# A two-role decoder layer on eight cores: the recurrent branch's convolution and gates of two equal tiles in one operation each

## The chip, the cores and the metric

The kernel runs on all eight cores of one Trainium2 chip. The cores do not talk to each other: each pair of cores serves one of the four sequences of the batch. The metric is the device time of the slowest core, in microseconds, and the number given for a kernel is the median of several executions.

## The reference

One decoder layer, x of shape (4, 4096, 1024) in float32:

```
h      = RMSNorm(x)
[u_pool | u_rnn | u_gate | g_pool | g_rnn] = h @ W_in
y_pool = PoolMixer(u_pool) @ W_pool_out
v      = conv4(u_rnn)                         # causal, depthwise, 4 taps
r, i   = sigmoid(v @ w_a + b_a), sigmoid(v @ w_x + b_x)     # 8 heads of 128x128
a      = exp(-8 r softplus(-lam));  h_t = a_t h_(t-1) + sqrt(1 - a_t^2) i_t v_t
y_rnn  = (h * gelu(u_gate)) @ W_rnn_out
x      = x + (sigmoid(g_pool) y_pool + sigmoid(g_rnn) y_rnn) @ W_o
x      = x + SwiGLU(RMSNorm(x));   out = RMSNorm(x)
```

## The kernel before

**Two roles.** Channels lie on the partitions, tokens on the free axis. An even core has role a: it computes the first 2240 tokens of its sequence. An odd core has role b: it computes the last 1856 tokens, but because the recurrence runs over the whole sequence it also runs norm, projection, convolution, gates and scan of the recurrent branch (and only these) over the 2240 tokens before its own. This part is called the prefix. Role a cuts its tokens in two chunks of three tiles each (256, 412, 396 and 344, 500, 332). Role b cuts the prefix in tiles of 256, 496, 496, 496, 496, taken in groups of 2, 2 and 1 tiles, and its own tokens in chunks of 508, 508 and 460, 380.

**The recurrent branch** is `rnn_group`, called for each of the eight heads (j = 0 to 7) and each group or chunk. For each tile of the group: eight matmuls of w + 4 columns into one PSUM bank (`proj`, L705); ScalarE evicts the bank with the fourth tap and the bias into `v` (L745); VectorE adds the other three taps, one operation each, reading the bank (L757); GpSimd, or ScalarE for some heads, casts `v` to bf16 (L765, L763); two matmuls with the head's gate weights (L770), and one tanh each on ScalarE into `th` and `wi` (L780). After the tiles of the group, one operation over all its columns for each of: exp (L788), square (L792 or L795), square root (L798), the product with v (L815), the product with the root (L822), and the scan (L828). Exp and tanh share one activation table, the square root needs another, so ACT_TABLE_LOADs stand between them.

**The rest of a chunk** is projections for the gelu (L993), pool and merge gates (L1012, L1027), the output projections, and the channel mixer, all matmuls through `mm_group` (L705) with one eviction or two each.

**Who sets the order.** Nothing is ordered by hand. Every operation gets a key, `base + step * block + toff * tile + off[block]`, from the tables in `ROLES`; a planner (`Planner.run`) walks a modelled time, lets each engine take the ready operation of lowest key, gives it SBUF and one of eight PSUM banks, and so fixes each engine's order, which the engines then follow strictly with semaphore waits. All numbers of `ROLES` come from a search over that model.

**The head.** Both roles begin with the same operations: the load of the first tile `xt` (SP queue), its norm, and on the GpSimd queue the loads of the projection weights of head 0, of all gate weights, and of heads 1 to 3:

```
            if j == 0:
                head.append(self.load("pool", rg, lambda: rg.tensor[:], dr["rg"], 128 * 2048 * 4, K, "rg"))
```

Weights are read as float32 and written as bf16 (a 512 KB `keep_rg` is 1 MB of reads). After the head each engine reads the role and branches into the stream of its role.

## Time and profile before

| | |
|---|---|
| median of 3 runs | 1024.84 us (1024.12 to 1025.46) |
| the profiled execution | 1024.35 us |
| its span on the slowest core, core 3 (role b) | 1022.8 us |
| PE, DVE, ACT, POOL busy on core 3 | 924.4, 591.4, 556.7, 336.8 us |
| mean granted TensorE clock, role a / role b | 0.985 / 0.951 to 0.954 |

The span runs from the first to the last instruction of a core; 1.55 us of the profiled execution lie outside the slowest span. PE is busy 90% of core 3's span, but the share is uneven: the first third has idle stretches and a clock below full, the last two thirds none. VectorE and ScalarE are the other way round.

### The profile page before, as it was taken

The page shows a single profiled execution, that of the slowest core. Times are in us where ns is not written, and L with a number is a line of the kernel's source. Part 1 is how long each engine was busy: PE and PEld are TensorE (multiplying, and loading weights), DVE is VectorE, ACT ScalarE, POOL GpSimd, SP SyncE. Part 2 cuts the span into 40 slices and gives each one's busy share as a digit, 9 for nine tenths or more (in the row PEclk, how much of TensorE's full clock was granted, in tenths as well). Part 3 has the DMA queues.
Part 4 walks back from the last instruction along what each step waited for, and adds up shares of the span by engine and source line. Part 5 has one row for each costly group of instructions (what it writes and reads, how often), then busy time and mean ns, then how long its engine had stood idle before and what let it go on. Part 6 is the DMA issues. An engine that isn't in the chain of part 4 may idle for free.

```text
span 1022.8 us, 13708 instructions; the slowest of 8 cores (1016.8 to 1022.8 us)
## 1 busy us (share of the span) xinstructions
PE 924.4 (90%) x4484; PEld 446.6 (44%) x4484; DVE 591.4 (58%) x798; ACT 556.7 (54%) x804; POOL 336.8 (33%) x347
## 2 busy tenths in 40 slices
PE   2378688698978999999999999999999999999995
PEld 1134233233433444444444444444555555555553
DVE  2179998999999867844253544533644452222235
ACT  2579997989889942548264938611722351111112
POOL 2438593778655641151001122112251211000000
PEclk8579789899989999999999999999999999999998
DMA  8921452003644276768403257255939175910003
GB/s 176 242 69 33 160 93 42 12 1 55 116 82 87 38 192 118 160 98 150 82 8 56 39 80 141 44 101 123 253 69 212 30 129 108 211 41 2 1 1 135
DMA packets 42765, 96.88 MB, mean 95 GB/s; under 512 B 3776, under 2 KB 19264, under 8 KB 42560
## 3 DMA queue, kind: packets, MB, share of 16 engines
q0 software_dynamic: 23904, 63.45, 36.1%
q1 hardware_dynamic: 18784, 32.48, 10.6%
q8 instruction: 40, 0.66, 0.2%
q14 instruction: 37, 0.30, 0.1%
HBM read 151.75 MB, written 7.60 MB: 156 GB/s over the span
## 4 chain that ended last, share of the span: by engine, by line
PE 78%; ACT 9%; issue 5%; POOL 3%; DVE 2%; DMA 2%; ACTq 0%; DVEq 0%; SPq 0%; POOLq 0%
PE bank L705 74%; PE bank L770 2%; PE bank L667 2%; DMA wu<-w_in 2%; ACT th L780 1%; DVE v L757 1%; ACT q L798 1%; POOL sq L638 1%; ACT th L788 1%; ACT v L745 1%; ACT L798 1%; ACT L780 1%; DMA xt<-xT 1%; POOL vb L765 1%; ACT wi L780 0%
## 5 line engine op out<-in xcount | busy, mean ns | idle before, releaser
L705 PE MATMUL bank<-h,wf 128*128 128x508 bf16 (+2 forms) x1408 | 280.7, 358 | 0.0
L705 PEld LDWEIGHTS bank<-h,wf 128*128 128x128 bf16 x1408 | 136.5, 97 | 139.9 <-issue 0.8
L757 DVE SCALAR_TENSOR_TENSOR v<-bank,keep_cst,v 128x496 f32<-128x496 f32 (+3 forms) x200 | 128.8, 683 | 32.4 <-POOL v L754 13.4
L705 PE MATMUL bank<-h,wu 128*128 128x500 bf16 (+4 forms) x576 | 130.1, 381 | 16.3 <-DMA wu<-w_in 11.0
L1084 DVE TENSOR_TENSOR ff<-tf,bank 128x508 bf16<-128x508 f32 (+2 forms) x88 | 55.7, 634 | 147.9 <-PE bank L705 123.5
L705 PE MATMUL bank<-ff,wz 128*128 128x508 bf16 (+2 forms) x704 | 139.5, 359 | 0.0
L1079 ACT ACTIVATE tf<-bank 128x508 f32<-128x508 f32 (+2 forms) x88 | 48.8, 557 | 137.8 <-PE bank L705 134.4
L652 ACT ACTIVATE sq<-x 128x508 f32<-128x508 f32 (+2 forms) x56 | 32.9, 590 | 125.3 <-DVE x L1096 97.4
L705 PEld LDWEIGHTS bank<-ff,wz 128*128 128x128 bf16 x704 | 68.9, 98 | 68.6 <-issue 0.5
L705 PEld LDWEIGHTS bank<-h,wu 128*128 128x128 bf16 x576 | 58.7, 103 | 83.9 <-issue 32.9
L765 POOL CAST vb<-v 128x496 bf16<-128x496 f32 (+3 forms) x68 | 61.1, 905 | 61.4 <-DVE v L757 53.3
L770 PE MATMUL bank<-vb,keep_rg 128*128 128x496 bf16 (+4 forms) x144 | 43.2, 381 | 33.4 <-ACT th L780 10.1
L515 POOL DMA_DIRECT2D wf<-wfi x44 | 23.8, 549 | 147.1 <-PE bank L705 106.0
L795 POOL TENSOR_TENSOR q<-th 128x752 f32<-128x752 f32 (+3 forms) x31 | 56.9, 1843 | 37.8 <-ACT th L788 18.9
L682 DVE SCALAR_TENSOR_TENSOR h<-xt,keep_cst,bank 128x500 bf16<-128x500 f32 (+4 forms) x72 | 45.8, 686 | 30.8 <-ACT bank L674 29.7
L745 ACT ACTIVATE v<-bank,keep_cst 128x496 f32<-128x496 f32 (+3 forms) x72 | 51.7, 732 | 19.1 <-PE bank L705 18.0
L705 PE MATMUL bank<-h,wa 128*128 128x508 bf16 (+2 forms) x256 | 56.6, 367 | 3.0 <-ACT th L780 1.7
L1096 DVE TENSOR_TENSOR x<-bank,x 128x508 f32<-128x508 f32 (+2 forms) x32 | 20.4, 639 | 64.9 <-PE bank L705 64.6
L705 PE MATMUL bank<-h,wg 128*128 128x508 bf16 (+2 forms) x256 | 55.2, 367 | 2.8 <-ACT th L780 1.9
L780 ACT ACTIVATE th<-bank,keep_hb 128x496 f32<-128x496 f32 (+3 forms) x72 | 44.8, 639 | 22.1 <-PE bank L770 21.8
L638 POOL TENSOR_TENSOR sq<-sq,sq 128x1000 f32<-128x1000 f32 (+2 forms) x18 | 41.9, 2330 | 36.9 <-ACT sq L623 30.3
L705 PE MATMUL bank<-h,wb 128*128 128x508 bf16 (+2 forms) x256 | 53.9, 363 | 0.0
(103 smaller groups left out, 1311.7 us busy)
## 6 DMA issues: line engine op xcount, KB each, us to landing
wf<-wfi POOLq DMA_DIRECT2D x44, 512.0 KB, 9.5
wz<-wfo POOLq DMA_DIRECT2D x16, 704.0 KB, 10.1
xt<-xT SPq DMA_DIRECT2D x16, 500.0 KB, 8.6
wu<-w_in POOLq DMA_DIRECT2D x16, 256.0 KB, 13.7
xt<-xT SPq DMA_DIRECT2D x8, 512.0 KB, 21.1
wa<-w_in POOLq DMA_DIRECT2D x16, 256.0 KB, 5.9
wg<-w_in POOLq DMA_DIRECT2D x16, 256.0 KB, 5.4
wb<-w_in POOLq DMA_DIRECT2D x16, 256.0 KB, 5.5
```

What stands on the lines that cost most here:

```text
L638: self.ew(adds, 2 * w, key, lambda e, t=t: e.tensor_tensor(out=sq.tensor[:], in0=sq.tensor[:], in1=t.tensor[:], op=ALU.add), [sq, t], [sq] ...
L652: g.op("act", c_act(w), key, lambda e: e.activation(out=s.tensor[:], in_=x2[cc // 2].tensor[:, cc % 2, :], func=AF.Square), rd=[(x2[cc // ...
L682: g.op("dve", c_dve(w) + 0.04, key + 0.1 * kc, lambda e, kc=kc, b=b, o=o, h=h: e.scalar_tensor_tensor(out=o.tensor[:, h, :], in0=b.tensor[ ...
L705: last = e.matmul(p.tensor[:, 0:n], lhsT=wap(kc), rhs=rhs(kc), start=(kc == 0), stop=(kc == K - 1))
L745: g.op("act", c_act(w, 2), k, lambda e, p=p, o=o, w=w: e.activation(out=v.tensor[:, o:o + w], in_=p.tensor[:, HALO:HALO + w], func=AF.Iden ...
L757: g.op("dve", c_dve(w), k, lambda e, p=p, o=o, w=w, s=s: e.scalar_tensor_tensor(out=v.tensor[:, o:o + w], in0=p.tensor[:, HALO - s:HALO - ...
L765: cast = lambda e, vb=vb, o=o, w=w: e.tensor_copy(out=vb.tensor[:], in_=v.tensor[:, o:o + w])
L770: g.op("pe", c_mm(w) + 0.05, k + 1 + 0.3 * q, lambda e, pg=pg, q=q, vb=vb, w=w: e.matmul(pg.tensor[:, 0:w], lhsT=self.rg.tensor[:, q, j, : ...
L780: g.op("act", c_act(w, 1), k + 1 + 0.3 * q, lambda e, pg=pg, out=out, hcol=hcol, w=w: e.activation(out=out(), in_=pg.tensor[:, 0:w], func= ...
L795: g.op("pool", 0.09 + 0.0018 * W, k, lambda e: e.tensor_tensor(out=q2.tensor[:], in0=th.tensor[:], in1=th.tensor[:], op=ALU.mult), rd=allp ...
L1079: g.op("act", c_act(w), kf, lambda e, pg=pg, th=th, w=w: e.activation(out=th.tensor[:], in_=pg.tensor[:, 0:w], func=AF.Silu), rd=[pg], wr= ...
L1084: g.op("dve", c_dve(w), kf, lambda e, pu=pu, th=th, fb=fb, w=w: e.tensor_tensor(out=fb.tensor[:], in0=th.tensor[:], in1=pu.tensor[:, 0:w], ...
```

## The change

It does four things.

1. Where a group has exactly two tiles of the same width, and neither the PSUM variant (`ps`), nor the ScalarE tap (`tap`), nor the PE convolution (`pec`) is in use for the head, a new function `rnn_pair` takes the place of the per-tile loop. Both tiles' projections go to the two halves of a pair of neighbouring PSUM banks, and the first eviction, each of the three taps, the cast and each tanh become one operation over both tiles. The matmuls stay as they are.
2. The planner can give out an even-numbered pair of neighbouring banks (`ps2`). Single banks are taken by preference from pairs whose other bank is in use.
3. The gate weights are stored by head, and loaded in four pieces of two heads. Only the first piece is in the head; the other three are loads of their own with keys.
4. Every number of `ROLES` is searched anew. Role b's prefix groups become 1, 2, 2 tiles (256; 496, 496; 496, 496), and its own second chunk 420, 420; the last chunk's `ps` goes from 1 to 0, and its `tap` from 8 heads to 2. The tile widths of role a stay (256, 412, 396 and 344, 500, 332), and so does the split at token 2240.

```
+    def find_bank(self, b, t):
+        free = [self.bank_live[i] is None and self.banks[i][0] <= t for i in range(8)]
+        if b.space == "ps2":
+            c = [(max(self.banks[i][0], self.banks[i + 1][0]), i) for i in range(0, 8, 2) if free[i] and free[i + 1]]
+        else:
+            c = [(self.bank_live[i ^ 1] is None, self.banks[i][0], i) for i in range(8) if free[i]]
+        return min(c)[-1] if c else None
...
-        self.rg = rg = self.buf("keep_rg", [2, 8, 128], BF16)
+        self.rg = [self.buf("keep_rg", [2, 2, 128], BF16) for _ in range(4)]
...
             if j == 0:
-                head.append(self.load("pool", rg, lambda: rg.tensor[:], dr["rg"], 128 * 2048 * 4, K, "rg"))
+                head.append(self.load_rg(0, K))
...
+    def load_rg(self, i, key):
+        b = self.rg[i]
+        return self.load("pool", b, lambda: b.tensor[:], self.dr["rg"][:, 2 * i:2 * i + 2], 128 * 512 * 4, key, "rg")
...
-        for i, (h, w, part) in enumerate(tiles):
+        both = len(tiles) == 2 and tiles[0][1] == tiles[1][1] and not (ps or on[2] or on[5])
+        if both:
+            self.rnn_pair(j, tiles, wu, key, toff, v, th, wi, kk_vb)
+        for i, (h, w, part) in enumerate([] if both else tiles):
...
+    def rnn_pair(self, j, tiles, wu, key, toff, v, th, wi, cast):
+        g, cst = self.g, self.cst
+        w = tiles[0][1]
+        two = lambda b: b.tensor[:].rearrange("p (t w) -> p t w", t=2)
+        p = self.banks("ps_u")
+        for i, (h, _, part) in enumerate(tiles):
+            self.mm_group(p, w + HALO, wu, lambda kc, h=h: h[kc // 2].tensor[:, kc % 2, 0:w + HALO],
+                          [(h[kc // 2], kc % 2) for kc in range(8)], key + toff * i, "u", wap=lambda kc: wu.tensor[:, kc, :], half=i)
+        k = key + toff
+        pk, vk = [(p, 0), (p, 1)], [(v, 0), (v, 1)]
+        g.op("act", c_act(2 * w, 2), k, lambda e: e.activation(
+            out=two(v), in_=p.tensor[:, :, HALO:HALO + w], func=AF.Identity,
+            scale=cst.tensor[:, C_CW + 24 + j:C_CW + 25 + j], bias=cst.tensor[:, C_CB + j:C_CB + j + 1]),
+            rd=pk + [cst], wr=vk, tag="v0")
+        for s in (1, 2, 3):
+            g.op("dve", c_dve(2 * w), k, lambda e, s=s: e.scalar_tensor_tensor(
+                out=two(v), in0=p.tensor[:, :, HALO - s:HALO - s + w],
+                scalar=cst.tensor[:, C_CW + 8 * (3 - s) + j:C_CW + 8 * (3 - s) + j + 1], in1=two(v),
+                op0=ALU.mult, op1=ALU.add), rd=pk + [cst] + vk, wr=vk, tag="cv")
+        vb = self.buf("vb", [2 * w], BF16)
...
+        for q, hcol, dst in ((0, 0, th), (1, 8, wi)):
+            pg = self.banks("ps_g")
+            for i in range(2):
+                g.op("pe", c_mm(w) + 0.05, k + 1 + 0.3 * q, lambda e, pg=pg, q=q, i=i: e.matmul(
+                    pg.tensor[:, i, 0:w], lhsT=self.rg[j // 2].tensor[:, j % 2, q, :], rhs=vb.tensor[:, i * w:i * w + w], start=True, stop=True),
+                    rd=[vb, self.rg[j // 2]], wr=[(pg, i)], tag="gt")
+            g.op("act", c_act(2 * w, 1), k + 1 + 0.3 * q, lambda e, pg=pg, dst=dst, hcol=hcol: e.activation(
+                out=two(dst), in_=pg.tensor[:, :, 0:w], func=AF.Tanh, scale=0.5,
+                bias=self.hb.tensor[:, hcol + j:hcol + j + 1]), rd=[(pg, 0), (pg, 1), self.hb], wr=[(dst, 0), (dst, 1)], table=TANH, tag="th")
...
+        base, step = (P["rnn"][0] if P else prm["keys"][0]["rnn"])[:2]
+        for i in range(1, 4):
+            self.load_rg(i, base + step * 2 * i - prm["lead"])
...
-        prefix=[256, 496, 496, 496, 496], groups=[2, 2, 1], own=[[508, 508], [460, 380]], wp=261.84, window2=107.54,
+        prefix=[256, 496, 496, 496, 496], groups=[1, 2, 2], own=[[508, 508], [420, 420]], wp=322.07, window2=277.53,
```

## Rows read from the trace of the kernel before

**Rows 1.** Spans and granted clock by core: even cores role a, odd role b

```profile
core 0: 1017.9 us, clock 0.985
...
core 3: 1022.8 us, clock 0.951
...
core 6: 1021.7 us, clock 0.985
```

**Rows 2.** Busy time by stretch, core 3 (role b): stretch, length, engines, PEclk, DMA

```profile
20.00:60.00 40.00, 13.61 (x44) 6.23 (x42) 11.38 (x22) 20.69 (x30) 20.47 (x17) 0.50 0.91 227
60.00:342.00 282.00, 235.96 (x988) 99.77 (x987) 264.53 (x297) 249.60 (x349) 187.65 (x149) 0.91 0.31 62
342.00:1000.00 658.00, 656.67 (x3366) 329.10 (x3366) 298.23 (x442) 278.58 (x413) 125.69 (x173) 1.00 0.51 97
```

**Rows 3.** Who PE waited for, core 3, 60 to 342 us: total, times, longest

```profile
PE bank L770 <- ACT th L780: 10.1, 6, 3.7
PE bank L770 <- DVE v L757: 8.5, 5, 4.2
```

**Rows 4.** Groups of VectorE instructions by form, core 3: busy us, mean ns

```profile
L757 DVE SCALAR_TENSOR_TENSOR v<-bank,keep_cst,v 128x496 f32<-128x496 f32 x96 | 65.2, 720 | 3.8 <-ACT v L745 3.7
...
L828 DVE TENSOR_TENSOR_SCAN wi<-th,q 128x752 f32<-128x752 f32 x8 | 16.6, 2073 | 0.5 <-POOL q L822 0.5
...
L757 DVE SCALAR_TENSOR_TENSOR v<-bank,keep_cst,v 128x256 f32<-128x256 f32 x24 | 11.1, 475 | 12.7 <-ACT v L745 6.3 <-ACT ab L582 5.6
...
L828 DVE TENSOR_TENSOR_SCAN wi<-th,wi,q 128x496 f32<-128x496 f32 x8 | 11.0, 1372 | 0.0
```

**Rows 5.** VectorE in order of time, core 3: start, us

```profile
211.76 2.00 DVE L757 SCALAR_TENSOR_TENSOR v<-bank,keep_cst,v 128x496 f32<-128x496 f32 x3
```

**Rows 6.** Groups of ScalarE instructions by form, core 3

```profile
L745 ACT ACTIVATE v<-bank,keep_cst 128x496 f32<-128x496 f32 x32 | 24.0, 763 | 4.8 <-PE bank L705 4.6 <-POOL acc L640 0.2
L780 ACT ACTIVATE th<-bank,keep_hb 128x496 f32<-128x496 f32 x32 | 21.4, 673 | 6.7 <-PE bank L770 6.6
...
L780 ACT ACTIVATE th<-bank,keep_hb 128x256 f32<-128x256 f32 x8 | 3.8, 473 | 1.8 <-PE bank L770 1.6
```

**Rows 7.** ScalarE in order of time, core 3

```profile
203.16 0.68 ACT L780 ACTIVATE wi<-bank,keep_hb 128x496 f32<-128x496 f32 x1
203.72 0.77 ACT L745 ACTIVATE v<-bank,keep_cst 128x496 f32<-128x496 f32 x1
204.36 0.61 ACT L1012 ACTIVATE tp<-bank 128x508 f32<-128x508 f32 x1
```

**Rows 8.** Busy time by stretch, core 6 (role a)

```profile
20.00:60.00 40.00, 25.18 (x99) 13.57 (x97) 12.30 (x23) 17.39 (x28) 12.90 (x26) 0.77 1.08 193
60.00:115.00 55.00, 52.85 (x351) 33.76 (x350) 51.68 (x70) 46.59 (x87) 20.19 (x23) 1.00 0.21 41
115.00:1000.00 885.00, 885.00 (x5515) 539.63 (x5514) 451.18 (x687) 373.65 (x622) 178.38 (x223) 1.00 0.44 88
```

**Rows 9.** Start of core 6 in order of time, POOL and PE

```profile
8.90 0.53 POOL L515 DMA_DIRECT2D keep_rg<-rg  x1
...
18.80 1.89 PE L705 MATMUL bank<-h,wu 128*128 128x260 bf16 x8 [5.81 <-DMA wu<-w_in]
...
21.36 0.53 POOL L515 DMA_DIRECT2D wq<-w_in  x1 [10.35 <-issue]
...
25.05 1.89 PE L705 MATMUL bank<-h,wu 128*128 128x260 bf16 x8 [4.37 <-DMA wu<-w_in]
...
30.19 0.56 POOL L765 CAST vb<-v 128x256 bf16<-128x256 f32 x1
...
38.68 3.11 PE L667 MATMUL bank<-sq,keep_ones 128*128 128x416 f32 x4 [1.76 <-ACT sq L623]
```

**Rows 10.** Start of core 0 (role a) in order of time, POOL and PE

```profile
14.47 0.53 POOL L515 DMA_DIRECT2D wq<-w_in  x1 [3.28 <-issue]
...
24.11 1.89 PE L705 MATMUL bank<-h,wu 128*128 128x260 bf16 x8 [4.26 <-DMA wu<-w_in]
...
34.01 3.11 PE L667 MATMUL bank<-sq,keep_ones 128*128 128x416 f32 x4 [1.65 <-ACT sq L623]
```

More of the change, by code:

```diff
@@ L164, in can_alloc @@
                 continue
-            if b.space == "ps":
-                if not any(self.bank_live[i] is None and self.banks[i][0] <= t for i in range(8)):
+            if b.space != "sb":
+                if self.find_bank(b, t) is None:
                     return False
@@ L169, in can_alloc @@
                 n += b.nbytes
-        if room and any(b.space == "ps" and b.left is not None for b in o.bufs):
+        if room and any(b.space != "sb" and b.left is not None for b in o.bufs):
             room = 0
@@ L179, in do_alloc @@
             b.left = b.uses
-            if b.space == "ps":
-                c = [(self.banks[i][0], i) for i in range(8) if self.bank_live[i] is None and self.banks[i][0] <= t]
-                _, i = min(c)
-                self.bank_live[i] = b
-                b.off = i
-                extra += self.banks[i][1]
+            if b.space != "sb":
+                i = b.off = self.find_bank(b, t)
+                for x in range(i, i + (2 if b.space == "ps2" else 1)):
+                    self.bank_live[x] = b
+                    extra += self.banks[x][1]
             else:
@@ L198, in finish_refs @@
                 b.dead = max(u.end for u in b.users)
[L199 to L200 removed]
+                if b.space != "sb":
                     us = {}
@@ L203, in finish_refs @@
                         us[u.eng] = u
-                    self.banks[b.off] = (b.dead + self.prm["bank_lag"], list(us.values()))
+                    for x in range(b.off, b.off + (2 if b.space == "ps2" else 1)):
+                        self.bank_live[x] = None
+                        self.banks[x] = (b.dead + self.prm["bank_lag"], list(us.values()))
                 elif b.name.startswith("keep"):
```

91 lines of the change are left out of this document (48 added, 43 removed).

## The prediction

> **What bounds the kernel now.** I read the spans of all cores first, because the metric is the slowest core and the two roles run different programs. Role b ends at 1022.8 us; of role a, core 0 ends at 1017.9, and core 6 at 1021.7 [rows 1]. So role b sets the time, but only 1.1 us ahead of the slowest core of role a. Whatever the change takes off role b beyond 1.1 us counts only if role a comes down too. This is the main fact of the case.
>
> Next, busy time by stretch. In role b PE is full from 342 to 1000 us (656.7 of 658); before that it is not: from 60 to 342 us it is busy 236 of 282 us at a clock of 0.91, while VectorE is busy 264.5 and ScalarE 249.6 [rows 2]. That stretch is bound by VectorE, with ScalarE close behind: the prefix and the first chunk's convolution, gates and scans. What PE waits for in it is work of these two: the gate matmuls wait for a tanh to free a bank (10.1 us) and for the taps (8.5 us) [rows 3]. From 20 to 60 us role b has the opposite picture: VectorE is busy 11.4 of 40 us and the DMA engines 91% [rows 2]. Before 342 us a microsecond less of VectorE work is a microsecond less of PE loss; behind it nothing is to be had.
>
> In role a PE is full from 115 to 1000 us (885 of 885 us). Its loss lies at the start: 14.8 us idle and a clock of 0.77 from 20 to 60 us, and 2.1 us idle from 60 to 115 [rows 8].
>
> **The merged operations (role b only).** Role a always has three tiles in a group, so nothing merges there. In role b two prefix groups, the first own chunk and six heads of the second chunk merge: 8 + 8 + 8 + 6 = 30 pairs. The last six lie where PE is full, and are worth nothing on the path. The other 24 each save 3 tap operations on VectorE and 1 eviction and 2 tanh on ScalarE. The columns stay, so only the fixed part of an operation is saved. VectorE: 496 columns take 720 ns, 256 take 475, so a column costs (720 - 475) / 240 = 1.02 ns and the fixed part of a duration is 720 - 506 = 0.21 us [rows 4]. But neighbours overlap: three taps in a row take 2.00 us, which is 0.64 us from start to start, of which 0.51 is columns and 0.13 fixed [rows 5]. Bounds: 72 x 0.13 = 9.4 us and 72 x 0.21 = 15.1 us. I take 9.4, since the engine is full and works at the spacing. ScalarE: a column of the tanh costs (673 - 473) / 240 = 0.83 ns [rows 6], 0.41 us for 496; the spacing is 0.56 us for a tanh and 0.64 for the eviction [rows 7], so fixed parts of 0.15 and 0.23 us: 48 x 0.15 + 24 x 0.23 = 12.7 us. Both engines of that stretch are relieved by about the same, so neither takes the other's place. I expect the saving to come through: -9.4 us.
>
> What does a merge cost? The first tap waits for the second tile's projection, and the banks are held longer. A pair of u banks is held for 8 matmuls, one eviction of about 1.2 us and three taps of about 1.2 us: some 7 us, while VectorE has 282 us for 24 pairs, or 11.8 us for each. One pair of u banks, at most two, and two pairs for the gates fit into eight banks. No row shows such an operation across two banks; below, the nearest is that it runs at the same 1.02 ns a column (what I take); above, that it splits at the bank border and costs its fixed part twice, and then the saving is nothing. The trace also speaks for a loss here, in that PE's longest wait is for a tanh to free a bank (3.7 us) [rows 3]. By the Trainium skill ("Perfetto Trace Analysis", Optimizing Tensor Performance) independent matmul groups should rotate through different banks, so that one's evacuation overlaps the next group's matmuls; a pair halves the number of places to rotate through. That speaks against this change, and if each of the 24 pairs cost one such wait, the sum would be a loss. Rows 3 put all waits for a tanh of the gate matmuls at 10.1 us in 282, so I give it a small chance.
>
> **The groups 1, 2, 2.** The first group is now the 256-column tile alone, so its exp, root and scan can run while the DMA engines still bring the next tiles, between 20 and 60 us, where VectorE is idle 28.6 us [rows 2]. The scan alone of these columns costs (2073 - 1372) ns x 8 heads = 5.6 us of VectorE [rows 4], now in the full stretch. Between 0 and 5.6 us; GpSimd's squares for the second tile stand in the same queue, so I take half, -2.8 us. Role b comes to 1022.8 - 9.4 - 2.8 = 1010.6 us.
>
> **The gate weights in four.** 384 of the 512 KB leave the head. On core 6 the weights of head 0 are used at 18.80 us and those of head 1, which wait for their DMA, at 25.05 [rows 9]: 6.25 us for 512 + 256 KB. Half of that is gone: -3.1 us for the second projection, and with it for what follows. The pieces come back as three loads of 128 KB each; the fixed issue is 0.53 us each on the GpSimd queue [rows 9], in front of casts, 1.6 us together at most. Is the gain passed on? On core 6 the first cast waits until 30.19 us behind weight issues that begin at 21.36, because GpSimd stood still for 10.35 us after the head; on core 0 it stood 3.28 us [rows 9, 10]. Core 6 is late by 4.7 us at the second tile's statistics (38.68 against 34.01), and still by 3.8 at the end [rows 1, 9, 10]. So a microsecond at role a's start is about a microsecond at its end, and the spread of its four cores is made in the head. If the stall lasts as long as the head's loads are under way, fewer bytes shorten it; if not, the gain stays 0 for that core. I take 3.1 us for all of role a: core 0 at 1014.8, core 6 at 1018.6.
>
> **The order searched anew, role a.** No row prices it. Its room is what PE loses between 20 and 115 us: 14.8 + 2.1 us idle, and 0.23 x 25.2 = 5.8 us of slow clock, together 23 us, of which the load above takes 3. Below: nothing is regained, and a new order can lose as much as the 3.8 us by which one core of the same order now trails. Above: half of the remaining 20. I take -3, because at 24 us PE still waits for a DMA while the second tile's statistics, which need no weights, stand behind it in the order [rows 9]. Role a's slowest core: 1015.6 us.
>
> **Sum.** Slowest core max(1010.6, 1015.6) = 1015.6, and the 1.5 us outside the span: 1017.1, so 1017. The profiled execution took 1024.35 us with a span of 1022.8, 0.5 below the median of the runs; the sum is made against it. The time is then role a's, and 5 us of role b's gain are hidden.
>
> **Rivals.**
> - *Role b keeps the end.* A merge returns little: operations that cross a bank border pay twice, or PE waits for two free neighbours. With 0 to 3 us of saving role b ends at 1019.8 to 1022.8, the time 1021.3 to 1024.3. For it: no such operation in the trace. Against: VectorE is busy 94% there, so removed instructions must show. Taken at 1022.
> - *Role a does not move.* The stall after the head is not made by the loads, and the weights are only read in another order: core 6 stays at 1021.7, the time 1023.2, within 0.2%. For it: two cores with the same head stand 3.3 and 10.4 us. Against: the wait for the second weights is a DMA wait on both.
> - *Both gain more.* The new order fills role a's start (half of 20 us): role a 1008.6, role b 1010.6 or lower, the time 1008 to 1012.
> - *Slower: neighbouring banks.* PE, with operations of both tiles in one bank pair, waits at the gates of each pair. The margin is 12.2 us of saving and 2.05 us more up to 0.2% over the median: at 14.3 / 24 = 0.6 us a pair it is slower. At the 1.7 us that a wait for a tanh lasts today (10.1 / 6) [rows 3] it would be +40.8 - 12.2 = +28.6 if all pairs met it, and with half of them +8, a time of 1033. This is what the rule of the Trainium skill on rotating through banks (named above) would come to here.
>
> **How the numbers follow.** Role a sets it near 1017: 0.50 (1012 to 1021). Role b keeps the end: 0.15. Role a does not move: 0.12. Both gain more: 0.13. Slower by the banks, or by an order of role a that loses over 3 us: 0.10. About 0.2% (2.05 us) is what a measurement can tell from no change, so below 1022.8 is faster: 0.50 + 0.13 + two thirds of 0.15 + a small part of 0.12 = 0.75; within 0.2%: 0.14; slower 0.11. The range takes in most of "both gain more" and ends where slower begins to be likely: 1007 to 1024.
>
> **What would show it.** Right: on odd cores, half as many operations at the taps, of 992 columns, at 1.2 to 1.25 us each, and PE full from about 330 us instead of 342; the odd cores' spans below the even ones'; on even cores the second projection at about 21 to 22 us. Wrong: taps of 992 columns at 1.4 us, which is twice 720 ns; long waits of L705 or L770 for a tap or tanh; PE idle behind 342 us in role b; even cores at 1017 and more.

## The result and the profile after

The change makes the kernel slower: 1041.65 us, the median of 6 executions (1040.20 to 1042.72), beside 1024.91 us before. The ratio is 1.0160, with a 95% interval of 1.0147 to 1.0173. The forecast was 1017 us (1007 to 1024). Where "role a" or "role b" is given a time below, it is the mean span of the four even or the four odd cores over the executions of that kernel; such a mean repeats within some 1.5 us (one and the same program of role a gave 1014.1 and 1012.6 in z1 and z3 below), single terms of that size are at its edge, and the kernel before itself stood 2 to 3 us higher beside z4 and z5 than elsewhere. Executions in which the cores of one die ran slower are left out everywhere. By these means role a goes from 1018.6 to 1020.7, and role b from 1021.3 to 1037.2 us.

The spans of the profiled execution after (1041.87 us), by core:

```profile
core 0: 1027.1 us, clock 0.982
...
core 3: 1040.3 us, clock 0.949
...
core 6: 1022.7 us, clock 0.986
```

All of the loss is role b's: core 3 ends 17.5 us later than in [rows 1]. Role a has not come down on core 6 (1021.7 before) and core 0 is 9 us later in this execution, though role a's mean is only 2.1 us up. The stall of GpSimd behind the head, which stood on core 6 before [rows 9], stands on core 0 this time (3.28 us there before [rows 10]):

```profile
21.64 0.53 POOL L527 DMA_DIRECT2D wu<-w_in  x1 [10.34 <-issue]
```

The same three stretches of core 3 as in [rows 2]:

```profile
20.00:60.00 40.00, 10.56 (x50) 6.50 (x50) 12.78 (x25) 22.41 (x33) 24.12 (x25) 0.63 0.82 173
60.00:342.00 282.00, 236.26 (x975) 98.75 (x976) 251.81 (x218) 229.49 (x272) 153.81 (x123) 0.90 0.34 72
342.00:1000.00 658.00, 647.45 (x3290) 320.63 (x3288) 305.84 (x408) 276.38 (x381) 122.23 (x157) 0.99 0.48 95
```

VectorE is busy 12.7 us less in the second stretch and ScalarE 20.1 us less, as a merge should make it; but PE is busy no more than before (236.3 against 236.0). The engines were relieved and the stretch was not shortened. Behind 342 us, PE is now idle 10.5 of 658 us, where it was idle 1.3. The merged operations themselves, core 3, 60 to 342 us, VectorE by form:

```profile
L876 DVE SCALAR_TENSOR_TENSOR v<-bank,keep_cst,v 128x992 f32<-128x992 f32 x48 | 58.2, 1240 | 2.2 <-ACT v L871 1.3
L847 DVE TENSOR_TENSOR_SCAN wi<-th,wi,q 128x992 f32<-128x992 f32 x16 | 44.0, 2754 | 8.6 <-POOL q L841 8.5
...
L834 DVE SCALAR_TENSOR_TENSOR wi<-wi,v 128x992 f32<-128x992 f32 x16 | 23.4, 1459 | 1.3 <-ACT wi L892 1.3
```

A tap of 992 columns across two banks takes 1240 ns, in the window that the prediction gave (1.2 to 1.25 us): no operation pays twice at a bank border. What stands below it is new: the scan of 992 columns takes 2754 ns, and the 16 scans together are kept 8.5 us by GpSimd's product L841. The same two operations before, same view and stretch (these rows stand in none of the groups above):

```profile
L828 DVE TENSOR_TENSOR_SCAN wi<-th,wi,q 128x992 f32<-128x992 f32 x8 | 19.1, 2400 | 0.0
...
L815 DVE SCALAR_TENSOR_TENSOR wi<-wi,v 128x992 f32<-128x992 f32 x8 | 10.1, 1277 | 0.0
```

**Where role b's time went.** The last product `gl` (L838 before, L857 after) of role b's first own chunk is the point behind which VectorE no longer holds PE. Before it starts at 364.5 us. After, the timeline of core 3, VectorE and then PE, shows it at 375.3:

```profile
372.85 2.33 DVE L847 TENSOR_TENSOR_SCAN wi<-th,keep_hst,q 128x1016 f32<-128x1016 f32 x1
375.29 1.22 DVE L857 TENSOR_TENSOR gl<-wi,gl 128x1016 bf16<-128x1016 f32 x1
...
369.75 1.66 PE L721 MATMUL bank<-h,wb 128*128 128x508 bf16 x7
376.76 5.48 PE L721 MATMUL bank<-gl,wr 128*128 128x508 bf16 x15 [5.34 <-DVE gl L857]
```

PE has nothing left to do in its order that does not need `gl`, and stands 5.34 us: the chain runs through VectorE up to here. The windows from 20 us to this point, and from it to 1000 us, before and then after:

```profile
20.00:364.50 344.50, 272.07 (x1136) 116.27 (x1134) 291.44 (x330) 291.42 (x409) 218.87 (x175) 0.87 0.39 83
364.50:1000.00 635.50, 634.17 (x3261) 318.82 (x3260) 282.70 (x431) 257.45 (x382) 114.94 (x163) 1.00 0.51 97
```

```profile
20.00:375.30 355.30, 275.23 (x1152) 117.64 (x1152) 290.51 (x259) 279.38 (x341) 191.46 (x156) 0.87 0.39 80
375.30:1000.00 624.70, 619.04 (x3161) 308.24 (x3162) 279.93 (x391) 248.89 (x345) 108.71 (x147) 1.00 0.50 98
```

The span after is 17.5 us longer: 10.8 us up to this point and 6.7 us behind it. Up to it VectorE is busy 291.4 us before and 290.5 after: the saving on the taps (9.7 us, 108.7 against 87.8 + 11.2) was given back inside other operations. And it is idle 53.1 us before, 64.8 after. What lies behind the point is settled further down, by z1. Who VectorE waited for up to it, after:

```profile
DVE h L698 <- ACT bank L690: 13.2, 2, 12.6
DVE wi L847 <- POOL q L841: 11.3, 3, 5.0
DVE v L776 <- ACT ab L598: 10.9, 1, 10.9
DVE v L776 <- ACT v L764: 8.5, 3, 6.3
DVE wi L834 <- ACT wi L892: 5.8, 4, 2.9
```

And three of the same waits before, 20 to 364.5 us:

```profile
DVE h L682 <- ACT bank L674: 24.0, 4, 17.4
DVE v L757 <- ACT ab L582: 5.6, 1, 5.6
DVE wi L828 <- POOL q L822: 2.8, 3, 2.3
```

Of the 11.7 us more of idle time, 8.5 are the scans' wait for a GpSimd product (2.8 to 11.3). The waits for ScalarE are 4.3 us more in all (46.2 to 50.5): the first tap waits longer (5.6 to 10.9), the norm of the later tiles less (24.0 to 13.2). The experiments ask what of all this is the merge, the pieces, the order, and the rule for single banks, which the prediction did not cost.

### The profile page after: what moved, and what is told of

Same layout as the page of the kernel before. It is cut to its first block, busy times and chain, and to the rows that moved or that the text cites. A ratio compares the mean times of both kernels' runs of the same rounds, so it can differ in the third digit from the quotient of the medians.

```text
span 1040.3 us, 13139 instructions; the slowest of 8 cores (1021.5 to 1040.3 us)
## 1 busy us (share of the span) xinstructions
PE 929.2 (89%) x4484; PEld 445.8 (43%) x4484; DVE 592.5 (57%) x694; ACT 540.7 (52%) x705; POOL 303.2 (29%) x312
## 3 DMA queue, kind: packets, MB, share of 16 engines
q1 hardware_dynamic: 18784, 32.48, 10.4%
## 4 chain that ended last, share of the span: by engine, by line
PE 78%; ACT 7%; DVE 6%; issue 5%; POOL 2%; DMA 2%; DVEq 0%; ACTq 0%; SPq 0%; POOLq 0%
PE bank L721 75%; DMA wu<-w_in 1%; DVE wi L847 1%; DVE h L698 1%; PE bank L889 1%; PE bank L683 1%; POOL sq L654 1%; ACT q L817 1%; ACT wi L892 1%; ACT th L892 1%; DVE v L876 1%; ACT th L807 1%; DMA xt<-xT 1%; DVE q L841 0%; ACT L817 0%
## 5 line engine op out<-in xcount | busy, mean ns | idle before, releaser
L721 PE MATMUL bank<-h,wf 128*128 128x508 bf16 (+1 forms) x1408 | 280.8, 358 | 2.9 <-DVE h L698 1.9
L1142 DVE TENSOR_TENSOR ff<-tf,bank 128x508 bf16<-128x508 f32 (+1 forms) x88 | 55.8, 637 | 175.9 <-PE bank L721 140.2
L721 PE MATMUL bank<-h,wu 128*128 128x500 bf16 (+3 forms) x576 | 131.2, 385 | 23.7 <-DMA wu<-w_in 11.4
L721 PE MATMUL bank<-ff,wz 128*128 128x508 bf16 (+1 forms) x704 | 139.5, 359 | 0.4 <-issue 0.2
L876 DVE SCALAR_TENSOR_TENSOR v<-bank,keep_cst,v 128x992 f32<-128x992 f32 (+2 forms) x90 | 107.4, 1216 | 13.5 <-ACT v L871 11.1
L814 POOL TENSOR_TENSOR q<-th 128x992 f32<-128x992 f32 (+2 forms) x31 | 52.7, 1701 | 59.8 <-ACT th L807 46.5
L841 POOL TENSOR_TENSOR q<-q,wi 128x992 f32<-128x992 f32 (+3 forms) x24 | 50.0, 2091 | 47.0 <-ACT q L817 35.4
L721 PE MATMUL bank<-h,wb 128*128 128x508 bf16 (+1 forms) x256 | 55.7, 370 | 8.1 <-ACT th L892 6.6
L834 DVE SCALAR_TENSOR_TENSOR wi<-wi,v 128x992 f32<-128x992 f32 (+3 forms) x40 | 48.7, 1223 | 18.4 <-ACT wi L892 12.6
L721 PE MATMUL bank<-gl,wr 128*128 128x508 bf16 (+1 forms) x256 | 53.7, 369 | 5.7 <-DVE gl L857 5.3
L721 PE MATMUL bank<-h,wg 128*128 128x508 bf16 (+1 forms) x256 | 56.0, 374 | 1.6 <-ACT wi L892 1.0
L721 PE MATMUL bank<-h,wa 128*128 128x508 bf16 (+1 forms) x256 | 54.5, 359 | 0.1
## 6 DMA issues: line engine op xcount, KB each, us to landing
wz<-wfo POOLq DMA_DIRECT2D x16, 704.0 KB, 10.9
```

Source lines behind the costliest of these rows:

```text
L721: last = e.matmul(p.tensor[:, 0:n] if half is None else p.tensor[:, half, 0:n], lhsT=wap(kc), rhs=rhs(kc), start=(kc == 0), stop=(kc == K ...
L814: g.op("pool", 0.09 + 0.0018 * W, k, lambda e: e.tensor_tensor(out=q2.tensor[:], in0=th.tensor[:], in1=th.tensor[:], op=ALU.mult), rd=allp ...
L834: g.op("dve", c_dve(w), k, lambda e, o=o, w=w, x=x: e.scalar_tensor_tensor(out=x(), in0=x(), scalar=1.0, in1=v.tensor[:, o:o + w], op0=ALU ...
L841: self.ew(on[1], W, k + 2, lambda e: e.tensor_tensor(out=q2.tensor[:], in0=q2.tensor[:], in1=wi.tensor[:], op=ALU.mult), [q2] + xk, [q2], "b")
L876: g.op("dve", c_dve(2 * w), k, lambda e, s=s: e.scalar_tensor_tensor(out=two(v), in0=p.tensor[:, :, HALO - s:HALO - s + w], scalar=cst.ten ...
L1142: g.op("dve", c_dve(w), kf, lambda e, pu=pu, th=th, fb=fb, w=w: e.tensor_tensor(out=fb.tensor[:], in0=th.tensor[:], in1=pu.tensor[:, 0:w], ...
```

## The experiments

### The merge and the pieces, each by itself

*x1* keeps the order of after and issues each merged operation per tile, back to back. *x5* does the same with finer waits: each tile's operation waits only for its own tile. *x3* exchanges the first two weight loads in the GpSimd queue. *y2* puts the pieces alone into the kernel before, the three late ones right behind the head.

```
# x1 (the eviction, the cast and the tanh alike)
-            g.op("dve", c_dve(2 * w), k, lambda e, s=s: e.scalar_tensor_tensor(
-                out=two(v), in0=p.tensor[:, :, HALO - s:HALO - s + w],
...
+            g.op("dve", c_dve(2 * w), k, lambda e, s=s: [e.scalar_tensor_tensor(
+                out=two(v)[:, i, :], in0=p.tensor[:, i, HALO - s:HALO - s + w],
...
# x5
+        o = first[m.idx] = Op(m.eng, m.dur / 2, m.key, lambda e, f=f: f(e, 0))
+        m.fn = lambda e, f=f: f(e, 1)
# x3
+    pl.order["pool"][pos[0]], pl.order["pool"][pos[1]] = b, a
# y2
-                head.append(self.load("pool", rg, lambda: rg.tensor[:], dr["rg"], 128 * 2048 * 4, K, "rg"))
+                head.append(self.load("pool", rg, lambda: rg.tensor[:, 0:2], dr["rg"][:, 0:2], 128 * 2048 * 4, K, "rg"))
...
+        pl.order["pool"].insert(at + i - 1, o)
```

> The order of the kernel after, with every merged operation (eviction, taps, cast, two tanh) issued as one for each tile, back to back, in the same place; the matmuls, banks, loads and all else stay. Theory 1, the merge gains on VectorE as forecast and something else loses: the spans of role b (odd cores, 1039.5 to 1040.3 in the kernel after) grow by about 24 heads x 3 taps x 0.13 to 0.20 us = 9 to 14 us on VectorE, less what still waits for other things: 1046 to 1055. Theory 2, the merge itself is what costs (a tile waits for its neighbour): the same places and waits are kept here, so the span stays within 3 us of 1040 or falls.

> The kernel after with each merged operation issued as one for each tile in the same place, as in x1_undone_in_place (role b 1048.7 in the mean), but now each tile's operation waits only for its own tile: the eviction of the first tile for its own projection, its taps for its own eviction, its gate matmuls for its own cast, its tanhs for its own gate matmuls. Theory 1, what a pair costs is its number of operations and columns, not that a tile waits for its neighbour: role b is within 2 us of x1. Theory 2, the waiting for the neighbour is what the order lost by: role b is 5 us or more below x1, which is then a cost of the merge that x1 does not show.

> The kernel after with the first two weight loads exchanged: the weights of head 1, which role b projects first, are issued ahead of head 0's. All orders on the engines stay. In the kernel after they land at 25.01 us and the first eviction of role b starts at 28.52. Theory 1, the late start is carried to the end: the first eviction starts 5 us earlier and role b ends at 1034 to 1036. Theory 2, the slack of the later stages takes it up: the first eviction starts earlier and the spans of role b stay at 1038 to 1041. Role a, which projects head 0 first, may lose 2 to 3 us and stays below role b.

> The kernel before with only the gate weights loaded in four pieces: the first where the whole load stood, the other three right behind the four weight loads of the start; every order on the engines, and all else, stays. Theory 1, the prediction's: head 1's weights land 3 us earlier and role a ends up to 3 us earlier (1015 to 1017 where the kernel before has 1017.5 to 1021), role b 1 us or less. Theory 2, the pieces only trade places with what is loaded beside them: the second projection starts 1 to 2 us earlier, the pieces for the later heads or the weights behind them land later, and the spans of both roles stay within 1 us.

| kernel | ratio to before (95%) | role a | role b |
|---|---|---|---|
| x1, per tile, waits of the pair | 1.0248 (1.0224 to 1.0272) | 1020.3 | 1048.7 |
| x5, per tile, waits of the tile | 1.0206 (1.0188 to 1.0224) | 1019.9 | 1041.0 |
| x3, head 1's weights first | 1.0141 (1.0119 to 1.0162) | 1022.4 | 1035.1 |
| y2, pieces in the kernel before | 0.9995 (0.9985 to 1.0005) | 1018.7 | 1019.9 |

Beside after's 1037.2 for role b, fewer operations are worth 11.5 us (x1), which is between the two bounds for VectorE (9.4 and 15.1); x1 also undoes the merges on ScalarE and GpSimd. But 7.7 us of that is paid back because a pair waits for both tiles (x1 to x5), so the merge's net worth in this order is 3.8 us. (With each kernel against the runs of before made beside it, the three numbers are 10.9, 6.8 and 4.1.) The order was searched with the pairs in it, and x1 and x5 keep it and the pairs of banks: in an order searched without them the merge may be worth something else. The taps of x1, same view as above:

```profile
L876 DVE SCALAR_TENSOR_TENSOR v<-bank,keep_cst,v 128x496 f32<-128x496 f32 x96 | 64.2, 722 | 3.1 <-ACT v L871 2.2
```

*x3*: the new order asks first for the weights that land second. The first projection of core 3, after and then x3:

```profile
25.25 4.87 PE L721 MATMUL bank<-h,wu 128*128 128x260 bf16 x24 [11.43 <-DMA wu<-w_in]
```

```profile
18.79 1.89 PE L721 MATMUL bank<-h,wu 128*128 128x260 bf16 x8 [5.24 <-DMA wu<-w_in]
24.45 1.89 PE L721 MATMUL bank<-h,wu 128*128 128x260 bf16 x8 [3.77 <-DMA wu<-w_in]
```

6.5 us earlier at the start is 2.1 us at the end. (1035.1 lies within the first theory's 1034 to 1036, but that was reckoned from the profiled execution of after, 1039.5 to 1040.3; from the mean it is less than half of the 5 us.) *y2*: the pieces alone are worth nothing measurable for the kernel; role b gains 1.4 us, which is at the edge of what can be told, and role a nothing (+0.4). In the profiled executions the second projection of the four even cores starts at 24.8 us in the mean before and at 22.5 in y2, but the second tile's statistics (L667 before) start at 35.7 before and 35.6 in y2. Core 0 and core 6 of y2, GpSimd and span:

```profile
20.01 1.59 POOL L1167 DMA_DIRECT2D keep_rg<-rg  x3 [8.68 <-issue]
15.14 1.59 POOL L1167 DMA_DIRECT2D keep_rg<-rg  x3 [3.88 <-issue]
core 0: 1023.3 us, clock 0.983
core 6: 1018.1 us, clock 0.985
```

The two cores have changed places: with a stall of 8.7 us in place of 3.3 core 0 ends 5.4 us later than before, with 3.9 in place of 10.4 core 6 ends 3.6 us earlier. In these traces the stall falls on another core in another execution, the end of a core of role a follows it, and the smaller load does not take it away.

### GpSimd and VectorE

*c1* (from after) and *c2* (from before) take from GpSimd the reading of its operands: squares and casts become memsets, products and sums have 8 columns. Values are therefore wrong in both, and GpSimd is also busy for less time (60 to 342 us: 79.4 us in place of 153.8 in c1, 84.1 in place of 187.7 in c2). *c3* shortens only the two products that stand beside the longest scan.

```
# c1, c2
-            g.op("pool", 0.09 + 0.0018 * W, k, lambda e: e.tensor_tensor(out=q2.tensor[:], in0=th.tensor[:], in1=th.tensor[:], op=ALU.mult),
+            g.op("pool", 0.09 + 0.0018 * W, k, lambda e: e.memset(q2.tensor[:], 0.01),
...
# c3
+        if o.idx in (713, 755):
...
+            o.fn = lambda e, q=q, x=x: e.tensor_tensor(out=q.tensor[:, 0:8], in0=q.tensor[:, 0:8], in1=x.tensor[:, 0:8], op=ALU.mult)
```

> The kernel after with GpSimd's reading left out: its squares and casts are memsets of the same size, its products and sums have 8 columns (so the values are not those of the reference); every order and wait stays. Theory 1, the operations of VectorE that only touch SBUF are stretched by GpSimd's and this eats the merge's gain: the scans of 992 columns fall from 2.75 us to about 2.3, VectorE's busy time in 60 to 342 us by 10 us or more, and role b ends below 1032, a fall at least 5 us larger than that of the same cut in the kernel before. Theory 2, the stretch is no matter: the fall is at most 3 us larger than in the kernel before.

> The same cut in the kernel before. Theory 1 (the stretch is a matter of the kernel after): the scans, 2.40 us for 992 columns, fall to about 2.3, and role b (1022.8) ends at 1018 to 1022. Theory 2: it falls by as much as the kernel after with the cut.

> The kernel after with only two of GpSimd's products (the two beside one scan of 992 columns in role b, at 309.5 and 314.0 us of core 3, 2.3 us each) cut to 8 columns; nothing else changes (so two heads' values are wrong). In the kernel after that scan takes 6.54 us where another of its size beside no work of GpSimd takes 2.27. Theory 1, VectorE and GpSimd take turns at SBUF and VectorE's operation waits inside its own time: the scan falls to 2.3 us and role b ends 3 to 4.5 us earlier (1035 to 1037 where the kernel after has 1039.5 to 1040.3). Theory 2, the scan is slow for another reason or the delay is taken up later: it stays long, or it falls and role b ends within 1 us of before the cut.

c1: ratio 1.0053 (1.0032 to 1.0073), role b 1026.9, 10.3 us below after. c2: 0.9944 (0.9927 to 0.9962), role b 1014.9, 6.4 us below before's 1021.3. c3: 1.0141 (1.0116 to 1.0166), role b 1035.5. VectorE of c1, same view and stretch:

```profile
L876 DVE SCALAR_TENSOR_TENSOR v<-bank,keep_cst,v 128x992 f32<-128x992 f32 x48 | 58.4, 1243 | 4.1 <-ACT v L871 3.3
L847 DVE TENSOR_TENSOR_SCAN wi<-th,wi,q 128x992 f32<-128x992 f32 x16 | 36.3, 2275 | 7.0 <-POOL q L841 6.9
...
L834 DVE SCALAR_TENSOR_TENSOR wi<-wi,v 128x992 f32<-128x992 f32 x16 | 18.9, 1180 | 4.8 <-ACT wi L892 4.8
```

Without GpSimd's reads the scan falls from 2754 to 2275 ns and the product with `v` from 1459 to 1180, while the tap, whose one large operand is in PSUM, stays at 1240. So GpSimd's work costs both kernels, and after 3.3 to 3.9 us more than before: 10.3 against 7.0 (by the runs of before made beside c2) or 6.4 (by their mean above). That lies between the two theories (at least 5 us more, at most 3 us more), so neither is borne out; and it prices all of GpSimd's work, the waits for its products included, not the stretched operations alone. One case shows how an operation is stretched; the timeline of after, and then of c3:

```profile
309.49 6.84 POOL L841 TENSOR_TENSOR q<-q,wi 128x992 f32<-128x992 f32 x3
...
311.88 6.54 DVE L847 TENSOR_TENSOR_SCAN wi<-th,wi,q 128x992 f32<-128x992 f32 x1 [5.01 <-POOL q L841]
```

```profile
312.71 2.29 DVE L847 TENSOR_TENSOR_SCAN wi<-th,wi,q 128x992 f32<-128x992 f32 x1 [6.86 <-POOL q L841]
```

The scan of after is charged 6.54 us, of which 2.3 are its own: it stands until GpSimd's three products, issued back to back, are done. In c3 the next scan starts 3.4 us earlier (316.10 against 319.51), and role b ends 1.7 us earlier: less than the 3 to 4.5 expected, and at the edge of what can be told.

### The clock at the start

*f1* and *f2* put matmuls with no use into PE's idle time of role b, in after and in before.

```
+                    for _ in range(n):
+                        last = e.matmul(t, lhsT=w[:, 0:128], rhs=w[:, 0:256], start=True, stop=True)
```

> The kernel after with extra matmuls of 256 columns on the gate weights in role b, where its order leaves TensorE idle over 1 us: six places, at most 2.0 us each (five before 60 us, one at 351), into the bank that the next group is to fill; nothing reads them. In the kernel after TensorE's granted clock in role b is 0.63 in 20 to 60 us and 0.78 in 60 to 100. Theory 1, a part of role b's loss is matmuls at the lower clock after idle stretches: with the idle partly filled the clock from 20 to 100 us rises and role b (mean over the runs 1037.2) ends 2 to 6 us earlier. Theory 2, the clock does not matter there, since VectorE sets the pace, or the extra matmuls delay the real ones: role b ends within 1 us or later.

> The kernel before with such extra matmuls in role b at four places, 2.0, 1.4, 7.5 and 7.5 us, all before 60 us; there TensorE's granted clock is 0.50 and it is busy 13.6 of 40 us. Theory 1: the clock is at its upper level from about 40 us on, and role b (mean 1021.5) ends 2 to 4 us earlier. Theory 2: the second tile's start is bound by its loads, and role b stays within 1 us or is later by what the extra matmuls delay.

f1: 1.0159 (1.0141 to 1.0177), role b 1037.7. f2: 0.9992 (0.9982 to 1.0002), role b 1020.5. Core 3 from 20 to 60 us in f2:

```profile
20.00:60.00 40.00, 28.61 (x191) 20.34 (x191) 11.25 (x22) 19.93 (x29) 20.26 (x17) 0.84 0.93 228
```

The granted clock rises from 0.50 [rows 2] to 0.84, and role b ends 0.6 us earlier than in the runs of before made beside it. In f1 it rises only from 0.63 to 0.69 there, and from 0.78 to 0.87 between 60 and 100 us, with nothing at the end. In that stretch of before PE waits for GpSimd (10.5 us for the sum and 3.6 for casts), ScalarE (7.5) and a load (4.8), which a higher clock does not bring forward. And after has the higher clock from 20 to 60 us and is the slower kernel. The clock there is not the cause.

### The order, and the rule for single banks

*s1* and *s2* use the code of after, with role a's order of before and role b's order searched anew near that of before, with the pairs merged (s1) or not (s2).

```
+                c = (o.key + pen, o.idx) if self.ref is None else (o.alloc, o.idx)
```

> The kernel before (its order of role a, its whole load of the gate weights, its groups 2, 2, 1) with merged operations in role b where two tiles of a group are equally wide (8 prefix pairs and 8 of the first chunk) and an order of role b searched from that of before with a model of VectorE and GpSimd taking turns. Theory 1, the merge is a gain and the order after lost it: with 16 pairs x 3 taps x 0.11 to 0.13 us = 5 to 6 us less on VectorE role b ends at 1014 to 1021 (before: 1021.3 in the mean); the kernel's time is then role a's, 1021 to 1024. Theory 2, merged operations cost in any order: role b ends above 1024.

> The control of s1_searched_merge: the kernel before with an order of role b searched in the same way, no merged operation. Theory 1 (the order alone can move role b by as much as the merge): role b differs from 1021.3 by 3 us or more to either side. Theory 2 (orders searched from the one before are worth the same): within 2 us.

s1: 1.0092 (1.0074 to 1.0111), role a 1028.9, role b 1030.3. s2: 1.0074 (1.0056 to 1.0092), role a 1029.2, role b 1027.4. These two say little of the merge (s1's role b is 2.9 us above s2's, but the orders differ, and both carry the rule for single banks of after, so that s1's 1030.3 does not bear out the theory that merges cost in any order). What they showed was not what they were made for: role a has here the order of before to the last instruction on each engine, and is 10 us slower. Of its program only the bank that each operation gets is different. The rule for single banks was the suspect, and the next two runs change it alone:

```
# z1, from after
-            c = [(self.bank_live[i ^ 1] is None, self.banks[i][0], i) for i in range(8) if free[i]]
+            c = [(self.banks[i][0] > t - 3.0, self.bank_live[i ^ 1] is None, self.banks[i][0], i) for i in range(8) if free[i]]
# z2, from before
-                c = [(self.banks[i][0], i) for i in range(8) if self.bank_live[i] is None and self.banks[i][0] <= t]
+                c = [(self.bank_live[i ^ 1] is None, self.banks[i][0], i) for i in range(8) if self.bank_live[i] is None and self.banks[i][0] <= t]
```

> The kernel after with one line of its planner changed: a single PSUM bank is no longer taken by preference next to an occupied one, whenever it was freed, but only from those free for 3 us at least (the banks' places change; the orders on the engines stay, but for two pairs of neighbours in role b). In s2_searched_no_merge role a had the order of before to the last instruction, but the bank choice of after, and ended at 1029.2 in the mean where before has 1018.6; TensorE fell behind step by step, from 1.1 us at its 1000th weight load of core 0 to 10.6 at its 6000th. Theory 1, the choice of a just freed bank costs TensorE about 1% wherever it sets the pace: role a, now 1020.7 in the mean, ends at 1009 to 1014, and role b, now 1037.2, at 1029 to 1034. Theory 2, that loss came from something else in that kernel: both roles stay within 2 us.

> The reverse in the kernel before: every order stays, only the rule for a single bank becomes that of the kernel after. Theory 1: role a goes from 1018.6 to about 1028, role b from 1021.3 to 1027 to 1031. Theory 2: within 2 us of before.

z1: 1.0104 (1.0089 to 1.0118); role a 1014.1 (6.6 below after), role b 1030.2 (7.0 below). z2: 1.0064 (1.0050 to 1.0079); role a 1028.4 (9.7 above before), role b 1026.4 (5.3 above). In z2 no engine's order differs from before; in z1 those of role a are those of after, and in role b PE's and ScalarE's differ in a few places. PE of core 0 from 400 to 1000 us, and its weight loads' waits, in before, after, z1 and z2:

```profile
400.00:1000.00 600.00, 600.00 (x3648) 356.67 (x3647) 289.38 (x438) 231.86 (x383) 96.41 (x131) 1.00 0.40 78
PEld bank L705 <- issue: 2.1, 9, 0.3
```

```profile
400.00:1000.00 600.00, 598.83 (x3627) 352.76 (x3626) 277.62 (x425) 229.83 (x376) 98.60 (x134) 1.00 0.41 80
PEld bank L721 <- issue: 9.5, 31, 1.2
```

```profile
400.00:1000.00 600.00, 600.00 (x3653) 357.30 (x3651) 278.18 (x432) 224.72 (x372) 96.25 (x132) 1.00 0.41 80
PEld bank L721 <- issue: 2.5, 11, 0.3
```

```profile
400.00:1000.00 600.00, 598.31 (x3609) 350.22 (x3607) 284.35 (x429) 230.96 (x380) 96.41 (x131) 1.00 0.40 77
PEld bank L705 <- issue: 12.1, 36, 0.8
```

PE counts as full in all four (598.3 to 600.0 of 600 us, clock 1.00), and yet does fewer matmuls in the same 600 us where the rule of after chooses banks: z2 1.1% fewer than before with the same orders (3609 against 3648), after 0.7% fewer than z1 (3627 against 3653). All four traces hold the same number of matmuls of this core to within one, so these are not records that are missing. The rule gives a matmul group a bank that was freed a moment ago, since it prefers the neighbour of a bank in use; the rule of before gives the one free for longest. The price is spread in small stalls that show as waits of the weight loads, and in no wait of PE of note (0.8 us in all in z2).

The same rule is what lies behind the last `gl` in role b. Core 3 of z1, the start of its last `gl`, and its span:

```profile
368.30 1.22 DVE L857 TENSOR_TENSOR gl<-wi,gl 128x1016 bf16<-128x1016 f32 x1
core 3: 1027.6 us, clock 0.957
```

From there to the end are 659.3 us, on all four odd cores. In after they are 664.5 to 665.1, in before 658.3 to 658.9, and in z2, which is before with the rule of after, 662.8 to 664.4. So nearly all of the 6.7 us that the kernel loses behind this point is the choice of single banks, and the 10.8 us up to it are mainly the order, less what the merge gives.

### Put together

*z3* has role a's order of after, role b's order of before without pairs, the pieces, and the rule of z1. *z4* adds the filling of f2. *z5* is x5 with the rule of z1.

```
-        both = len(tiles) == 2 and tiles[0][1] == tiles[1][1] and not (ps or on[2] or on[5])
+        both = self.prm.get("merge", True) and len(tiles) == 2 and tiles[0][1] == tiles[1][1] and not (ps or on[2] or on[5])
...
-        prefix=[256, 496, 496, 496, 496], groups=[1, 2, 2], own=[[508, 508], [420, 420]], wp=322.07, window2=277.53,
+        prefix=[256, 496, 496, 496, 496], groups=[2, 2, 1], own=[[508, 508], [460, 380]], wp=261.84, window2=107.54,
```

> Role a with the order of the kernel after, role b with the order of the kernel before (no merged operation), the gate weights in four pieces in both, single banks by the rule of z1_after_banks_rested. Theory 1 (the new order of role a is a gain that the bank choice hid; role b's new order is the loss): role a ends at 1009 to 1014, role b at 1018 to 1021, the time 1021 to 1023.5 and faster than before by 0.1 to 0.4%. Theory 2 (role a's new order is worth nothing): role a at 1017 or more, the time no better than before's.

> z3_after_a_before_b with the extra matmuls of f2_before_filled in role b (four places before 60 us). If the gains add, role b, 1018.4 in z3, ends 0.8 us earlier and the time is 0.4% under before's; if f2's 0.8 us was no gain, nothing changes against z3.

> z1_after_banks_rested with the merges undone and each tile waiting only for itself, as in x5_undone_fine. If the effects add, role b ends at 1041.0 - 7.0 = 1034, which is 3.8 us above z1 (1030.2): the merge's net worth in this order. Against role b of the kernel before with its weights in four pieces (1019.9) the rest, 14 us, is then the new order and groups of role b with no merge, no bank choice and no load in it. If the waits for the neighbour only mattered because banks were scarce, the two come out alike.

z3: 0.9965 (0.9951 to 0.9979), 0.35% faster than before; role a 1012.6, role b 1018.4. z4: 0.9963 (0.9949 to 0.9977), not told from z3. z5: 1.0136 (1.0108 to 1.0164). Beside z4 and z5 the runs of before stood higher (role b 1023.3), so role b is taken against them: z5 +15.4, z4 -3.1 (z3: -2.8). The same difference is +9.1 for z1, so with rested banks the merge is worth 6.3 us. The effects do not simply add: z5 was expected at 1034, some 13 us above before, and the rested banks take 4.6 us off x5 but 7.0 off after. The end of the stretch that VectorE sets is at 357.3 us on core 3 of z3:

```profile
357.33 1.22 DVE L866 TENSOR_TENSOR gl<-wi,gl 128x1016 bf16<-128x1016 f32 x1
```

## Why the prediction was wrong

**What was right.** Taps of 992 columns at 1240 ns; 9.7 us off VectorE's taps against 9.4; no double price at a bank border. VectorE does set role b's first third, and behind it nothing was gained, only lost. The even cores' second projection: 21.93 us on core 0 and 22.40 on core 6, against "about 21 to 22".

**The step that failed first: role b's new order was priced by its groups alone (-2.8 us), and the merge's saving was passed on 1:1.** The sum gave role b 1010.6; it ended at 1040.3. By the means, role b lost 15.9 us to before. The steps from one kernel to the next in role b:

| term | forecast | measured |
|---|---|---|
| weights in pieces (y2) | nothing | -1.4 |
| order, groups, tile widths (y2 to z5) | -2.8 | +16.8 |
| merge (z5 to z1) | -9.4 | -6.3 |
| rule for single banks (z1 to after) | not in the sum | +7.0 |
| together | -12.2 | +16.1 (directly: +15.9) |

z5 has no merged operation and rested banks, and ends 15.4 us above before; less the pieces, the order with its groups and widths costs 16.8 us. (z5 still keeps the pairs of banks, in an order searched for merges, and an error of 2 us in either mean is possible.) Two parts can be named: about 2 us for the order in which the first weights are asked for (x3), and 3 to 4 us more for GpSimd's work (c1, c2; this compares whole kernels, so some of it may be the merge's). No run divides the other 11 us, nor parts the order from the groups 1, 2, 2. Their place can be told: up to the last `gl`, core 3 of z5 and then of y2:

```profile
20.00:380.50 360.50, 274.80 (x1152) 117.24 (x1152) 296.67 (x330) 291.36 (x412) 202.14 (x180) 0.87 0.40 81
20.00:358.00 338.00, 267.24 (x1137) 114.75 (x1136) 291.80 (x330) 291.39 (x409) 219.50 (x178) 0.89 0.40 84
```

VectorE is busy 4.9 us more and idle 17.6 us more; it waits 9.8 us more for GpSimd's products (12.6 against 2.8). Over the four odd cores the last `gl` of z5 starts 18.2 us later than that of y2 (376.6 against 358.4 in the mean), and the very first tap already starts 5.2 us later (28.5 against 23.2). So the new order starts late by some 5 us and keeps VectorE waiting for most of the rest; why stays open.

**The merge: right in sign, too large, and not the slow part.** The prediction took 9.4 us, an engine's saving passed on whole. The smaller number of operations was worth 11.5 (x1), but waiting for the neighbouring tile takes 7.7 of it, leaving 3.8 us, or 6.3 with rested banks (z1, z5). The clause "the first tap waits for the second tile's projection" was there, and was priced at nothing. Nor is a microsecond of VectorE a microsecond of the end, as the prediction had it for the time before 342 us: in c1 VectorE is busy 18.5 us less from 60 to 342 us (233.3 against 251.8), and role b ends 10.3 us earlier.

**The rule for single banks was in the diff and not in the sum.** The prediction weighed the rotation of banks only for pairs. It also moves every single bank, in role a too, where no pair exists: +9.7 us there and +5.3 in role b in z2; -6.6 and -7.0 in z1. The rule of the Trainium skill that it named ("Perfetto Trace Analysis", Optimizing Tensor Performance: independent groups should rotate through different banks) agrees with these runs, and it has no price; here it is about 1% of PE's full stretch. The prediction named that rule for the pairs alone and gave it a small chance.

**Role a.** The prediction took the slowest core from 1021.7 to 1015.6, 6.1 us down. With the bank rule put right, role a's mean does come down: 4.6 us in z1, 6.1 in z3. So the size of the sum was about right and the new rule hid it (+2.1 in after); no run has role a's new order with the rule of before, which would part the two fully. The division of the sum was wrong: the pieces, taken at -3.1, give +0.4 (y2), and the order gives what is seen. The failed link is "and with it for what follows": in y2 the second projection came 2.2 us earlier in the mean, the second tile's statistics not at all. That a microsecond at role a's start is about one at its end is borne out (core 0 of y2: statistics 5.0 us later, end 5.4 later), but what moves the start is the stall of GpSimd, which the smaller load does not shorten; the prediction had named that case ("if not, the gain stays 0 for that core"). The new order does move it: on cores with a stall of 3.1 to 3.3 us the statistics start at 34.0 and 34.5 us before, and at 31.7 and 31.8 after.

**The rivals.** "Slower: neighbouring banks" had the right sign, with a time of 1033, but not its mechanism: PE's longest group of waits for a tanh at the gates is 9.1 us, against 10.1 in [rows 3], from the page of waits, core 3, 60 to 342 us:

```profile
PE bank L889 <- ACT th L892: 9.1, 6, 4.5
...
PE bank L721 <- DVE v L876: 4.7, 2, 3.7
```

Its chance was shared with an order of role a that loses; that role b's order could lose stood in no rival, though it alone decided the case. Nothing in the profile of before forbade an order that loses 15 us, and the sum gave it no upper end at all. "Role b keeps the end" came true, but at 1040 us and not at 1022. "Role a does not move" came close to true (+2.1), for the rule for single banks, which it did not have.

## What to carry to other kernels

Read every line of a diff for whom it reaches: a helper's tie-break that exists for one new buffer kind here moved all banks of both roles and cost 5 to 10 us. When an edit comes with a newly searched order, give the order its own term with an end on the losing side, and try the edit in the old order first; the best kernel here (z3) keeps role a's new order and role b's old one. Where fewer, larger operations wait for more inputs, subtract the wait from the saving: here it took two thirds of it. And a start that stalls on one core of a role in one execution and on another in the next is not explained by one profile: read all cores of several executions before pricing it.

## What the runs showed of the hardware

**A VectorE operation with both operands in SBUF and a GpSimd operation that reads SBUF take turns**, and the wait stands inside the duration. The 992-column scan took 2275 ns without GpSimd's reads (c1), 2754 on average beside GpSimd and 6.54 us in one case, in which GpSimd's next product was issued back to back; the taps, which read PSUM, stayed at 1240. The Trainium skill ("SBUF — State Buffer", 🔬 SBUF: two separate sides) says that the pair of ports is an exclusive lock that is held for the whole instruction, and that a VectorE operation with two SBUF inputs needs it against a GpSimd operation that reads SBUF; the durations agree, for the scan too.

**Which PSUM bank a matmul group gets costs PE time that no wait of PE shows.** With equal orders PE did 1.1% fewer matmuls in 600 us (3609 against 3648), at full clock and a busy share of 99.7%. z1 still prefers a bank whose neighbour is in use, but only among those free for 3 us, and gets the time back; so I hold the time since the bank was freed for the cause. No run sets that time by itself.

**A higher clock at the start returned nothing**: 0.50 to 0.84 from 20 to 60 us (f2), 0.6 us at the end, while PE waited for GpSimd, ScalarE and loads.

**GpSimd stands for a varying time behind the head's loads, and role a's end follows.** With role a's program of before it stood 3.1 to 10.4 us in the eight core traces of before and f2. The four cores that stood up to 3.3 us ended at 1016.8 to 1019.0, the two that stood 9.0 and 10.4 at 1020.7 and 1021.7. No run shows what the stall is made of.
